# A decoder step on one core: TensorE's attention and search steps put ahead of the weighted sum of the same pick

## Chip, core and metric

The kernel runs on one core of one Trainium2 chip. The metric is the time of one execution on the device, in microseconds; the time of the kernel before is the median of 3 runs, 4178.97 us (4177.4 to 4180.96).

## What is computed

One layer of a decoder for a prompt of 1024 rows and 8 sample sequences of 8 rows. The rows go through a combined projection, an mLSTM group and a dilated attention group, an output projection, and then the part that most of the time goes to, a retrieval over 128 x 128 = 16384 experts of one neuron each. In the reference:

```python
K = PEER_TOPK                                     # 16, for each of 8 heads
s = jnp.einsum('nhpd,pkd->nhpk', qh, sub_keys)    # two times 128 sub-key scores
sv, si = lax.top_k(s, K)
cand = sv[:, :, 0, :, None] + sv[:, :, 1, None, :]
fv, fpos = lax.top_k(cand, K)                     # the best 16 of 256 pairs
gate = jax.nn.softmax(fv, axis=-1)
act = jax.nn.gelu(jnp.einsum('nd,nhkd->nhk', xblk, u_tab[eidx]), approximate=False)
return jnp.einsum('nhk,nhkd->nd', (gate * act), v_tab[eidx])
```

So each row has 8 x 16 = 128 picks, and a pick needs one row of `u_tab` (for a dot product) and one of `v_tab` (for a weighted sum), 1024 numbers each. All is float32.

## The kernel before

Three stages follow each other. Stage 0 makes conditioning rows and bias tables, stage 1 runs the projection and the mLSTM, and stage 3, which begins about 1000 us into the execution, does the attention, the output projection and the retrieval. The change is in stage 3.

**Windows and picks.** Stage 3 works on tiles of 128 rows, 8 of the prompt and a ninth of 64 sample rows. `windows` lists pairs (i, n): in window (i, n) tile i has its 128 picks, while the attention and the search of tile n = i+1 are done beside them. So there are: a first window with no picks of experts (the attention of the sample rows beside tile 0), eight windows i = 0 to 7 with both, and a last one, the 64 picks of tile 8 alone. In windows 0 to 6 tile n has an attention; in window 7 (n = 8) it has a search alone. The same loop over c, the pick, is written out in the program of every engine. It is the order of the statements in that loop that sets each engine's queue; there is no scheduler.

**One pick** of tile i, number g = 128 i + c:

- GpSimd (POOL, L1160) gathers 128 rows of 8 KB (u and v side by side, 1 MB in all) into slot g % 6 of a ring of 6. It waits until the sum of pick g - 6 is done.
- VectorE (DVE, L1631) waits for the slot and multiplies and adds up the u half with the row's input: one number for each of the 128 rows.
- ScalarE (ACT, L1441, L1442, L1445) applies gelu, multiplies by the gate and spreads the 128 weights on the diagonal of a 128 x 128 matrix. There are 4 such matrices; it waits until the sum of pick g - 4 is done.
- TensorE (PE, L1335) waits for the diagonal and multiplies it with the v half, adding up in two banks of PSUM: the weighted sum. Its end frees the slot.

**Steps beside the picks.** `slots(n)` gives the pick at which each step of tile n stands. Attention of a head that begins at pick f (f = 5, 8, 11, ... in windows 0 to 4, and 5, 9, 13, ... in windows 5 and 6): PE makes the scores at f (L1190 against the keys of earlier tiles, L1192 against its own), DVE adds the bias and finds the maximum at f+2 (L1474), ACT takes the exponent at f+3 (L1362, with a table load before it, and one after it for the gelu), PE transposes at f+4 (L1198), ACT copies at f+6 (L1368), PE multiplies with the values at f+7 (L1209, L1210), and DVE scales at f+9 (L1479, L1480). The keys and values of earlier tiles come by SyncE's DMAs, one pair of heads at a time into one buffer each (L1008 and L1014); a load of keys is issued only after the scores of the pair before, and stands in SP's queue behind the load of values, which waits for the products of that pair.

After the heads come a norm over the head outputs, the output projection (PE, two matmuls in each of eight picks, L1234), the residual (DVE, L1512 to L1515, at the fifth and sixth and the ninth and tenth pick after the projection begins), the norm of the result (ACT, L1383 to L1385, with three table loads from there to the next gelu), and then 16 queries (PE L1252, ACT L1391 two picks later, PE L1260 three picks later, DVE five picks later). A query's matmuls wait for the copy of the query before it.

In each pick, DVE and ACT first do the expert's part and then the step of the other tile. PE did the same: first the sum, then the step:

```python
pe.wait_ge(sig["diag"], g + 1)
for half in range(2):
    mm = nc.tensor.matmul(psum[0:r, half], diag[:, g % 4, 0:r], ring[:, g % N_SLOTS, 1, half * 512:(half + 1) * 512], ...)
mm.then_inc(sig["summed"], 1)
```

Of the kernel before, what the change touches and what calls it, by code (L numbers as in the profile page):

```python
# [23 lines left out]
NT = SEQ // P  # L24
# [841 lines left out]
def slots(n):  # L866

    at = {"load": 2}
    if n < NT:
        step = 3 if n < 6 else 4  # L870
        at["head"] = [at["load"] + 3 + step * hh for hh in range(H_B)]
        at["rms"] = at["head"][-1] + 9
        at["turn"] = at["rms"] + 4
    else:
        at["head"], at["rms"], at["turn"] = (), None, 12
    at["out"] = at["turn"] + 4
    at["x1"] = at["out"] + 5
    at["sq"] = at["out"] + 11
    at["h2"] = at["sq"] + 2
    at["turn2"] = at["h2"] + 2  # L880
    first = at["turn2"] + 4
    at["q"] = [first + j * min(45, 99 - first) // 15 for j in range(2 * HEADS)]
    at["found"] = found = [c + 5 for c in at["q"]]
    at["cand"] = [found[2 * hh + 1] + 1 for hh in range(HEADS)]
    at["cand2"] = [c + (2 if c + 1 in found else 1) for c in at["cand"]]
    at["place"] = at["cand2"][-1] + 1
    assert at["place"] + 14 < PICKS
    return at


def stage3(nc, block, sig, mem, psum, const, ins, outs, scratch):
# [76 lines left out]
    def rows_of(i):  # L968
        return NS if i == NT else P

    def picks_of(i):

        return HALF if i == NT else PICKS
# [191 lines left out]
    def _(pe):  # L1165
# [96 lines left out]
        def s_scores(b, p):  # L1262
            m = 3 * b + p
            _, w = S_PIECES[p]
            old = min(512, ROWS - 512 * p)
            if m == 0:
                pe.wait_ge(sig["s_qbd"], 8)
                pe.wait_ge(sig["s_kt"], 2)
            pe.wait_ge(sig[f"s_keys_in{m % 2}"], 16 * (m // 2 + 1))
            if m >= 2:  # L1270
                pe.wait_ge(sig["s_biased"], m - 1)
            for j in range(2):
                for a in range(2):
                    q = s_qbd[:, 2 * a + j, 32 * b:32 * b + 64]
                    mm = nc.tensor.matmul(psum[64 * a:64 * a + 64, m % 2, 0:old], q, s_keys[:, m % 2, 2 * a + j, 0:old], start=j == 0, stop=j == 1)
            if old < w:
                for j in range(2):
                    for a in range(2):
                        q = s_qbd[:, 2 * a + j, 32 * b:32 * b + 64]
                        mm = nc.tensor.matmul(psum[64 * a:64 * a + 64, m % 2, old:w], q, s_kt[a][:, j, DS * b:DS * b + DS], start=j == 0, stop=j == 1)  # L1280
            mm.then_inc(sig["s_s_ps"], 1)

        def s_values(b, g):
            m = 3 * b + g
            t0, n = S_GROUPS[g]
            pe.wait_ge(sig["s_probs_t"], m + 1)
            pe.wait_ge(sig[f"s_vals_in{m % 2}"], 16 * (m // 2 + 1))
            if g == 0 and b >= 1:
                pe.wait_ge(sig["s_o"], b)
            for t in range(t0, t0 + n):  # L1290
                for a in range(2):
                    cols = slice(256 * a, 256 * a + 256)
                    if t < KT_ROWS:
                        mm = nc.tensor.matmul(psum[64 * a:64 * a + 64, 3, 0:256], s_probs_t[:, t, 64 * a:64 * a + 64], s_vals[:, m % 2, t - t0, cols], start=t == 0, stop=False)
                    else:
                        pe.wait_ge(sig["s_new_in"], 16 * (b + 1))
                        mm = nc.tensor.matmul(psum[64 * a:64 * a + 64, 3, 0:256], s_probs_t[0:DS, t, 64 * a:64 * a + 64], s_new[0:DS, cols], start=False, stop=True)
            mm.then_inc(sig["s_o_part"], 1)

        def sample(c):  # L1300
            if c == 0:
                pe.wait_ge(sig["s_raw_in"], 16)
                for n in range(2):
                    for j in range(4):
                        tr = nc.tensor.transpose(psum[:, 0, n * 256 + j * NS:n * 256 + (j + 1) * NS], s_raw[:, n * W_B + j * P:n * W_B + (j + 1) * P], ident[0:NS, 0:NS])
                tr.then_inc(sig["s_turned_ps"], 1)
            for b, first in enumerate(S_FIRST):
                if first <= c < first + 3:
                    s_scores(b, c - first)
                for g, (t0, n) in enumerate(S_GROUPS):  # L1310
                    if c == first + 8 + 3 * g:
                        pe.wait_ge(sig["s_probs"], b + 1)
                        if 3 * b + g >= 1:
                            pe.wait_ge(sig["s_probs_t"], 3 * b + g)
                        for t in range(t0, t0 + n):
                            m = P if t < KT_ROWS else DS
                            tr = nc.tensor.transpose(psum[0:m, 2, (t - t0) * P:(t - t0 + 1) * P], s_probs[:, t * P:t * P + m], ident)
                        tr.then_inc(sig["s_pt_ps"], 1)
                    if c == first + 12 + 3 * g:
                        s_values(b, g)  # L1320

        for i, n in windows:
            at = None if n is None else slots(n)
            picks = picks_of(i)
            for c in range(picks):
                if i is None:
                    sample(c)
                if i is not None:
                    r = rows_of(i)
                    g = i * PICKS + c  # L1330
                    if c == 0 and i >= 1:
                        pe.wait_ge(sig["acc_read"], 2 * i)
                    pe.wait_ge(sig["diag"], g + 1)
                    for half in range(2):
                        mm = nc.tensor.matmul(psum[0:r, half], diag[:, g % 4, 0:r], ring[:, g % N_SLOTS, 1, half * 512:(half + 1) * 512], start=c == 0, stop=c == picks - 1)  # L1335
                    mm.then_inc(sig["summed"], 1)
                if n is not None and n < NT:
                    attention(n, c, at)
                if n is not None:
                    search(n, c, at)  # L1340

    @block.scalar
    def _(act):
# [378 lines left out]
```

## Time and profile before

| what | value |
|---|---|
| time, median of 3 runs | 4178.97 us |
| the profiled execution: its own time, its span | 4189.1 us, 4187.3 us |
| granted TensorE clock, mean | 0.94 |
| DMA, mean over the span | 339 GB/s |
| PE / DVE / ACT / POOL busy, share of the span | 84% / 57% / 39% / 31% |
| largest shares of the chain that ended last | PE weighted sum 21%, DMA of experts 20% |

The span is the time from the first to the last instruction of one profiled execution. That execution took 4189.1 us, 0.24% above the median of the runs shown. A busy share is an average over stages with different limits: what a change in one stage is worth has to be read from that stage. In the section of rows, a window is a stretch of the span in microseconds from its start, and a bracket at the end of a row of the timeline tells how long the engine was idle before the row and what released it.

### The profile page before, as it was taken

To read this page: it belongs to the slowest core of one execution; us is meant where nothing else is said; L and a number is where in the kernel's file an instruction comes from. 1 tells how busy PE (TensorE), PEld (TensorE's weight loads), DVE (VectorE), ACT (ScalarE), POOL (GpSimd) and SP (SyncE) were. 2 spreads that over 40 slices of the span, in tenths; PEclk is the share of its full clock that TensorE was granted. 3 is DMA by queue.
4 is the path that set the end of the run, shared out by engine and by line. 5 is a ranking of instruction groups with operands and counts; after the bars stand their busy time and mean duration, and the time that the engine had idled before them with its cause. 6 is when DMAs were issued, how large, how long until landed. Compare 5 with 4: busy or idle time off the path is not lost.

```text
span 4187.3 us, 38259 instructions
## 1 busy us (share of the span) xinstructions
PE 3507.9 (84%) x12228; PEld 1772.0 (42%) x12228; DVE 2391.9 (57%) x5587; ACT 1616.4 (39%) x4381; POOL 1283.8 (31%) x1204
## 2 busy tenths in 40 slices
PE   7299999678689879978987897898889789889877
PEld 1065665445335334433533453453445344425321
DVE  1044554326548746944874595478548656947744
ACT  0033233123443453454345444443543453333333
POOL 0000000011334433423442343344344334435433
PEclk9699999679799999998998999899999999999999
DMA  9796011875799999999998999899999999999998
GB/s 377 266 339 217 26 44 36 169 251 200 307 377 413 416 358 402 413 364 349 414 416 325 398 413 397 321 401 416 397 386 400 412 386 396 400 368 410 413 408 366
DMA packets 241245, 1420.21 MB, mean 339 GB/s; under 512 B 42963, under 2 KB 65875, under 8 KB 93315
## 3 DMA queue, kind: packets, MB, share of 16 engines
q0 software_dynamic: 168768, 1200.70, 71.4%
q1 hardware_dynamic: 68692, 132.05, 9.9%
q10 hardware_dynamic: 3584, 85.01, 5.7%
q8 instruction: 97, 1.59, 0.2%
q14 instruction: 104, 0.85, 0.1%
HBM read 1385.48 MB, written 98.73 MB: 354 GB/s over the span
## 4 chain that ended last, share of the span: by engine, by line
PE 32%; DMA 25%; DVE 11%; ACT 8%; issue 2%; POOL 1%; SPq 0%; ACTq 0%; POOLq 0%; DVEq 0%
PE psum L1335 21%; DMA mem<-in_experts,mem 20%; DVE mem L1631 6%; PE psum L1252 4%; PE psum L1234 3%; DMA mem<-key_cols 3%; ACT L1441 2%; DVE mem L1497 1%; ACT mem L1445 1%; DVE mem L1496 1%; ACT mem L1442 1%; DMA mem<-qkv_rows 1%; ACT L1362 1%; PE psum L1190 1%; ACT mem L1441 1%
## 5 line engine op out<-in xcount | busy, mean ns | idle before, releaser
L1335 PE MATMUL psum<-mem 128*128 128x512 f32 (+1 forms) x4352 | 2136.4, 624 | 376.9 <-ACT mem L1445 374.8
L1160 POOL DMA_INDIRECT mem<-in_experts,mem x1088 | 1218.0, 1120 | 1882.0 <-PE psum L1335 1814.7
L1631 DVE CUSTOM_DVE_ANT_0 mem<-mem 128x1024 f32<-128x1024 f32 x1088 | 1321.4, 1221 | 705.8 <-DMA mem<-in_experts,mem 694.5
L1335 PEld LDWEIGHTS psum<-mem 128*128 128x128 f32 (+1 forms) x4352 | 774.5, 193 | 1458.0 <-ACT mem L1445 733.4
L1441 ACT ACTIVATE mem<-mem 128x1 f32<-128x1 f32 x1088 | 219.3, 202 | 1579.1 <-DVE mem L1631 1574.6
L1445 ACT ACTIVATE mem<-mem 128x128 f32<-128x128 f32 (+1 forms) x1088 | 434.3, 399 | 35.7
L589 PE MATMUL psum<-mem 128*128 128x512 f32 (+3 forms) x864 | 342.7, 548 | 11.0 <-ACT mem L554 9.8
L1442 ACT ACTIVATE mem<-mem 128x1 f32<-128x1 f32 x1088 | 320.4, 294 | 35.3
L1252 PEld LDWEIGHTS psum<-mem 128*128 128x128 f32 x2304 | 274.4, 191 | 45.1 <-issue 41.7
L1252 PE MATMUL psum<-mem 128*128 128x128 f32 (+1 forms) x2304 | 282.1, 275 | 2.5 <-ACT mem L1391 2.5
L589 PEld LDWEIGHTS psum<-mem 128*128 128x128 f32 (+1 forms) x864 | 148.8, 190 | 178.4 <-issue 164.6
L471 POOL DMA_DIRECT2D qkv_rows<-mem x9 | 5.1, 563 | 563.6 <-DVE mem L811 563.6
L1474 DVE CUSTOM_DVE_ANT_0 mem<-psum,mem 128x128 f32<-128x128 f32 (+7 forms) x64 | 48.4, 757 | 192.3 <-PE psum L1192 180.0
L1496 DVE MAX8 mem<-mem 128x8 f32<-128x128 f32 (+3 forms) x432 | 146.1, 338 | 12.5
L1497 DVE FIND_INDEX8 mem<-mem 128x8 uint32<-128x128 f32 (+3 forms) x432 | 142.3, 330 | 0.0
L1190 PE MATMUL psum<-mem 64*128 64x512 f32 (+3 forms) x160 | 70.0, 545 | 79.9 <-DMA mem<-key_cols 79.9
L1234 PE MATMUL psum<-mem 128*128 128x512 f32 (+1 forms) x288 | 135.5, 594 | 0.0
L616 PEld LDWEIGHTS psum<-mem 128*128 128x128 f32 x1152 | 131.5, 194 | 7.7 <-issue 4.2
L616 PE MATMUL psum<-mem 128*128 128x128 f32 (+1 forms) x1152 | 131.9, 276 | 2.7 <-DVE mem L823 2.7
L315 PE MATMUL psum<-mem 128*9 128x512 f32 x192 | 91.3, 634 | 21.7 <-DMA mem<-in_norm_gain 14.1
L1441 ACT ACT_TABLE_LOAD x80 | 102.6, 1283 | 14.8 <-DVE mem L1631 13.5
L508 ACT ACTIVATE mem<-mem 128x1024 f32<-128x1024 f32 (+1 forms) x9 | 9.4, 1045 | 212.4 <-DMA mem<-in_x 212.4
(259 smaller groups left out, 2577.6 us busy)
## 6 DMA issues: line engine op xcount, KB each, us to landing
out_k_s<-in_cache_k ACTq DMA_DIRECT2D x8, 4080.0 KB, 104.5
out_v_s<-in_cache_v ACTq DMA_DIRECT2D x8, 4080.0 KB, 117.2
mem<-in_w_ada SPq DMA_DIRECT2D x12, 2048.0 KB
mem<-mod_rows SPq DMA_DIRECT2D x34, 512.0 KB
mem<-in_experts,mem POOLq DMA_INDIRECT x1088
mem<-in_keys_t POOLq DMA_DIRECT2D x16, 1024.0 KB, 6.5
mem<-in_vals POOLq DMA_DIRECT2D x16, 1024.0 KB, 7.7
mem<-in_w_in ACTq DMA_DIRECT2D x8, 1796.0 KB, 40.5
```

Of the source, the lines that this page charges most:

```text
L589: mm = nc.tensor.matmul(psum[0:rows, bank, at:at + n], h_ts[i % 2][:, k, 0:rows], w_in[:, k, col:col + n], start=k == 0, stop=k == KD - 1)
L616: mm = nc.tensor.matmul(psum[:, c // 4, c % 4 * P:c % 4 * P + rows], w_in[:, k, O_QK + c * P:O_QK + (c + 1) * P], h_ts[i % 2][:, k, 0:rows ...
L1160: pool.indirect_dma_start(out=ring[:, g % N_SLOTS].rearrange("p a n -> p (a n)"), out_offset=None, in_=ins["experts"][:, :], in_offset=bas ...
L1234: mm = nc.tensor.matmul(psum[0:r, out_banks(n)[half]], turned[:, k, 0:r], w_out[:, k, half * 512:(half + 1) * 512], start=k == 0, stop=k = ...
L1252: mm = nc.tensor.matmul(psum[:, 5, j % 4 * P:j % 4 * P + r], w_q[:, k, j * NKEY:(j + 1) * NKEY], turned[:, k, 0:r], start=k == 0, stop=k = ...
L1335: mm = nc.tensor.matmul(psum[0:r, half], diag[:, g % 4, 0:r], ring[:, g % N_SLOTS, 1, half * 512:(half + 1) * 512], start=c == 0, stop=c = ...
L1441: chain.link(a.activation(act_v[:, c:c + 1], dots[:, c:c + 1], ACT.Gelu))
L1442: chain.link(a.activation(weight[:, c:c + 1], act_v[:, c:c + 1], ACT.Copy, scale=gate[i % 2][:, c:c + 1]))
L1445: a.activation(diag[:, g % 4, 0:r], spread, ACT.Copy, scale=weight[:, c:c + 1]).then_inc(sig["diag"], 1)
L1496: chain.link(v.max(values[:, e:e + 8], src))
L1497: chain.step(v.max_index(places[:, e:e + 8], values[:, e:e + 8], src))
L1631: v.tensor_tensor_reduce(row, row, h2[i % 2], 1.0, 0.0, ALU.mult, ALU.add, dots[:, c:c + 1]).then_inc(sig["dots"], 1)
```

## The change

In PE's loop of stage 3 the two calls of the other tile's steps move ahead of the sum:

```diff
@@ PE, the loop over picks
             for c in range(picks):
                 if i is None:
                     sample(c)
+                if n is not None and n < NT:
+                    attention(n, c, at)
+                if n is not None:
+                    search(n, c, at)
                 if i is not None:
                     r = rows_of(i)
                     g = i * PICKS + c
@@
                     mm.then_inc(sig["summed"], 1)
-                if n is not None and n < NT:
-                    attention(n, c, at)
-                if n is not None:
-                    search(n, c, at)
```

So PE's queue was sum(c), step(c), sum(c+1), step(c+1), and is now step(c), sum(c), step(c+1), sum(c+1). The lines of the sum move from L1335 to L1339. The other engines' queues stay as they are.

PE's queue at the beginning of window 0, before (two rows of L1335 are one sum; L1174 and L1176 are the first step, at pick 2, and L1190 and L1192 the scores of heads 0 and 1, at picks 5 and 8):

```order
L1335 MATMUL psum<-mem 128x512 x6
L1174 MATMUL psum<-mem 128x128 x4
L1176 MATMUL psum<-mem 128x128 x4
L1335 MATMUL psum<-mem 128x512 x6
L1190 MATMUL psum<-mem 128x128
L1192 MATMUL psum<-mem 128x128
L1335 MATMUL psum<-mem 128x512 x6
L1190 MATMUL psum<-mem 128x128
L1192 MATMUL psum<-mem 128x128
```

The same place now:

```order
L1339 MATMUL psum<-mem 128x512 x4
L1174 MATMUL psum<-mem 128x128 x4
L1176 MATMUL psum<-mem 128x128 x4
L1339 MATMUL psum<-mem 128x512 x6
L1190 MATMUL psum<-mem 128x128
L1192 MATMUL psum<-mem 128x128
L1339 MATMUL psum<-mem 128x512 x6
L1190 MATMUL psum<-mem 128x128
L1192 MATMUL psum<-mem 128x128
```

Two sums instead of three stand ahead of the first step; from there on the rows are the same in kind and number, but every sum between two steps is that of one pick earlier.

PE's queue at the end of window 7, before (L1260 is the last of the search's matmuls, for the 64 rows of tile 8; the sums of 64 rows are the last window):

```order
L1335 MATMUL psum<-mem 128x512 x6
L1260 MATMUL psum<-mem 64x128
L1335 MATMUL psum<-mem 128x512 x88
L1335 MATMUL psum<-mem 64x512 x128
```

And now:

```order
L1339 MATMUL psum<-mem 128x512 x6
L1260 MATMUL psum<-mem 64x128
L1339 MATMUL psum<-mem 128x512 x90
L1339 MATMUL psum<-mem 64x512 x128
```

The sum that went missing at the beginning stands behind the last step here, 45 instead of 44.

## Rows read from the trace of the kernel before

**Rows 1.** The page: the span, and busy time of each engine.
```profile
span 4187.3 us, 38259 instructions
PE 3507.9 (84%) x12228; PEld 1772.0 (42%) x12228; DVE 2391.9 (57%) x5587; ACT 1616.4 (39%) x4381; POOL 1283.8 (31%) x1204
```

**Rows 2.** Stretches: us, busy us of five engines, PE clock, DMA share, GB/s. Windows 0 to 7.
```profile
1079.30:4013.40 2934.10, 2529.70 (x8008) 1244.20 (x8008) 1883.64 (x4314) 1290.37 (x3652) 1154.30 (x1023) 0.96 0.98 391
```

**Rows 3.** Stretches of window 2: heads, projection, norm, queries, tail; then the heads of window 5.
```profile
1810.90:1936.60 125.70, 92.36 (x266) 45.37 (x266) 55.23 (x115) 67.03 (x152) 35.61 (x34) 0.86 0.87 334
1936.60:1977.60 41.00, 41.00 (x106) 18.58 (x105) 20.06 (x35) 14.28 (x45) 15.59 (x15) 1.00 0.98 375
1977.60:2001.30 23.70, 17.95 (x41) 7.48 (x39) 10.61 (x16) 12.20 (x31) 9.94 (x9) 0.86 1.01 403
2001.30:2107.80 106.50, 104.45 (x453) 62.55 (x452) 92.97 (x281) 40.23 (x142) 46.55 (x41) 1.00 1.01 414
2107.80:2171.20 63.40, 49.84 (x102) 17.89 (x101) 49.08 (x89) 24.46 (x75) 27.27 (x25) 0.97 1.01 417
2944.90:3078.70 133.80, 115.33 (x382) 60.13 (x382) 67.06 (x130) 78.33 (x176) 47.30 (x41) 0.95 1.00 394
```

**Rows 4.** Who waited for whom, whole span: total us, times, longest us.
```profile
POOL mem L1160 <- PE psum L1335: 1814.7, 964, 16.2
PE psum L1335 <- ACT mem L1445: 374.8, 372, 20.7
DVE mem L1474 <- PE psum L1192: 180.0, 37, 15.2
PE psum L1190 <- DMA mem<-key_cols: 79.9, 14, 11.1
DVE mem L1512 <- PE psum L1234: 77.1, 18, 7.6
```

**Rows 5.** Timeline of window 2, projection to norm: start us, us, engine, line.
```profile
1970.60 1.88 PE L1234 MATMUL psum<-mem 128*128 128x512 f32 x4
...
1972.32 7.04 PE L1335 MATMUL psum<-mem 128*128 128x512 f32 x16
1972.52 0.69 DVE L1512 TENSOR_TENSOR mem<-psum,mem 128x512 f32<-128x512 f32 x1 [5.97 <-PE psum L1234]
...
1981.27 1.28 ACT L1441 ACT_TABLE_LOAD   x1
...
1983.59 8.62 PE L1335 MATMUL psum<-mem 128*128 128x512 f32 x13 [4.23 <-ACT mem L1445]
```

**Rows 6.** Timeline of PE in window 7, the same place.
```profile
3759.70 4.53 PE L1335 MATMUL psum<-mem 128*128 128x512 f32 x6 [4.02 <-ACT mem L1445]
```

**Rows 7.** Timeline of window 2, heads 4 to 6: a wait for keys.
```profile
1872.02 1.99 PE L1335 MATMUL psum<-mem 128*128 128x512 f32 x4 [0.59 <-ACT mem L1445]
...
1875.29 0.49 SPq L1008 DMA_DIRECT2D mem<-key_cols  x1
...
1888.04 1.61 PE L1190 MATMUL psum<-mem 64*128 64x384 f32 x2 [9.31 <-DMA mem<-key_cols]
...
1890.01 3.77 PE L1335 MATMUL psum<-mem 128*128 128x512 f32 x4
...
1894.05 0.94 POOL L1160 DMA_INDIRECT mem<-in_experts,mem  x1 [14.11 <-PE psum L1335]
```

**Rows 8.** Timeline of window 5, one head at 4 picks a head.
```profile
2983.22 0.19 ACT L1362 ACTIVATION_READ_ACCUMULATOR mem<-mem 128x1 f32 x1
...
2984.12 0.39 PE L1210 MATMUL psum<-mem 128*128 128x64 f32 x2
...
2985.74 3.66 PE L1335 MATMUL psum<-mem 128*128 128x512 f32 x4 [1.23 <-ACT mem L1445]
...
2989.19 0.99 PE L1198 MATMUL psum<-mem 128*128 128x128 f32 x7
```

**Rows 9.** Waits of PE alone in the heads of window 2.
```profile
PE psum L1335 <- ACT mem L1445: 14.1, 14, 3.4
```

## The prediction

> **What bounds the kernel now.** I read the page first. PE is busy for 84% of the span [rows 1], but that mixes three stages, so the next view is the stretch from the first sum of window 0 to the last of window 7: 2934.1 us of the 4187.3 in which the DMA engines move 391 GB/s [rows 2]. Then the same view stage by stage, for one window. In its tail, 20 picks and more with no step on PE, 63.4 us hold 25 gathers, 2.54 us each, at 417 GB/s [rows 3]. That is the pace that the transfers allow. The queries run at 414. The heads run at 334 and the projection at 375 [rows 3]; there the transfers starve, because slots come free too late. The share column hardly shows it (0.98 at 375 GB/s), the GB/s do. Had the whole stretch moved 417, it would be 2934.1 x (1 - 391/417) = 183 us shorter. No change of order can give more than that.
>
> Who frees slots late? The table of waits says that POOL waits for sums for 1814.7 us in all, and PE for diagonals for 374.8 us and for keys for 79.9 us [rows 4]. So there are places where PE, which has the sums to make, stands still. Those are the places to look at; the timeline shows three kinds.
>
> **What the change moves.** PE issues the same instructions in the same sequence of kinds. The first sum ahead of the first step is carried behind the last step, so that between two steps stand the sums of one pick earlier. A sum's place in the queue now needs a diagonal that is made one pick sooner. In return, a step is one sum nearer to the start, and the slot that a place in the queue frees is one pick older. Nothing is added: no DMA, no instruction, and the queues of ACT, DVE, POOL and SP do not change. The rule that I draw from it: wherever PE waits in a loop "step on PE, then work on DVE and ACT, then a diagonal, then a sum", the loop now has one more sum of PE inside the time it waits. Four sums in a row take 7.04 us [rows 5], so one is 1.76 us. Where PE waits for a DMA that itself hangs on a step, as many sums stand between the two steps as before, and nothing is won.
>
> **Term A, projection to norm, 8 windows.** The last matmuls of the projection end at 1970.60 + 1.88 = 1972.48 and release DVE, which had been stuck for 5.97 us with later dot products queued behind it. From there the chain goes over the residual, ACT's norm and three table loads, the last at 1981.27, to the next diagonal, and PE goes on at 1983.59 [rows 5]. That is 11.1 us, in which PE has 4 sums (7.04 us) and then idles for 4.23. Now it has 5. The idle time becomes 4.23 - 1.76 = 2.47 us. Window 7, which has no attention, shows the same wait with 4.02 us [rows 6]. The transfers are starved at this place (375 GB/s in the stretch before [rows 3]), so an earlier sum is an earlier gather. 8 x 1.76 = 14.1 us. Bounds: nothing, if the transfers that follow (403 to 414 GB/s) are late anyway; and twice that, 28 us, since the norm over the heads ahead of the projection has a like chain (a wait of 3.4 us is the longest one in the heads [rows 9]).
>
> **Term B, heads of windows 5 and 6.** Here a head takes four picks. PE ends its product at 2984.12 + 0.39 = 2984.51, and the exponent was ready at 2983.41. But the transposes that need the exponent stand behind the sum, the sum behind the diagonal, and the diagonal behind ACT's table load for the gelu: PE idles for 1.23 us, and then makes the sum, in 3.66 us [rows 8]. With the step first, PE takes the transposes and scores at once, and ACT's table load and diagonal run beside them. The wait goes. It comes once a head. Of eight heads I count five, as the transfers are still ahead in the first ones, at 1.0 us: the stretch moves 394 GB/s and has room for 133.8 x (1 - 394/417) = 7.4 us, whatever PE does [rows 3]. 2 windows x 5 x 1.0 = 10 us; bounds 0 and 2 x 7.4 = 14.8.
>
> **Term C, heads of windows 0 to 4.** The large loss here is the wait for keys. PE issues scores at 1888.04 after 9.31 us of idle time; the keys were sent for at 1875.29 [rows 7]. Two sums stand between the product that releases the load and the scores that need it, before and after, so the wait stays. What goes are the small waits between: 0.59 us at the sum just ahead of that product [rows 7]. This kind comes about four times a window in the loops of the keys and values. 5 windows x 4 x 0.6 = 12 us. Bounds: 0; and half of what PE waits there for diagonals without the longest, (14.1 - 3.4) / 2 = 5.4 a window, 27 in all [rows 9].
>
> **Costed at nothing.** The queries: PE is busy for 104.45 of 106.5 us, the transfers run at 414 of 417 [rows 3], so both are full and order is worth nothing. Half of the queries wait for a copy that ACT makes behind the diagonal of the same pick; now that sum stands behind the query. What hides it is that gathers run ahead; if that cover is gone it costs 0.3 to 2 us a query. The tail and the last 64 picks have no steps. Sum: 14.1 + 10 + 12 = 36 us. Against the profiled execution's 4189.1 us that is 4153 us; its median counterpart, 10 us lower, is 4178.97 - 36 = **4143 us**. What is late next is the keys, and the transfers' own 417 GB/s.
>
> **Rivals.** A measurement of this kernel can tell about 0.2%, 8 us, from no change.
>
> *The transfers bound it.* Then the starved places are made good by the bursts after them, and only idle time of PE changes: 4179 us, within 8. For it: in all eight windows the share of the DMA engines is 0.98 [rows 2]. Against it: 334 and 375 GB/s beside 417 [rows 3]. The Trainium skill's page Perfetto Trace Analysis (Roofline) names about 435 GB/s as what the 16 DMA engines of one core give together, and so speaks against any gain by order where that is reached; the trace agrees in the tail, with 417, and not in the heads.
>
> *The keys give it back.* The load of keys of [rows 7] lands 12.75 us after its issue, beside gathers that are released as sums go. If an earlier issue only meets more gathers in flight, term C is nothing and the rest stands: 4179 - 24 = 4155 us. The Trainium skill's page DMA: Bandwidth & Descriptors (Queues, rings and completion order) says that each DMA engine takes turns between its queues, a packet at a time, so that a small load lasts as long as its turns among others' packets; by that rule term C would be 0 here. No row here shows the turns themselves.
>
> *Slots come back one pick later.* During each of the 14 waits for keys [rows 4] the ring now holds one transfer less behind PE: the sum that used to be made ahead of the scores is behind them. If that is what starves the transfers afterwards (POOL waits 14.11 us at one, and the first sum runs for 3.77 us [rows 7]), each wait costs one pick of 2.54 us: 14 x 2.54 = 35.6 us, against A and B with 24: 4179 + 12 = **4191 us, slower**. It decides if scores come at the same time as before. Against it: the place in the queue at which the load is sent for is earlier by the same sum, so that the wait should move as a whole.
>
> *It reaches further.* If A comes at its double and B and C at their upper bounds, 28 + 15 + 27 = 70 us: 4109 us. For it: DVE waits 180 us for scores and 77.1 us for the projection [rows 4], with dot products stuck behind, and each of these waits gets a sum shorter.
>
> **How the numbers follow.** The forecast, with its terms off by up to a half (4125 to 4161), gets 0.53; the keys 0.12; the further reach 0.11; the transfers as the bound 0.13; later slots 0.11. Faster by over 0.2%: 0.53 + 0.12 + 0.11 = 0.76; within: 0.13; slower: 0.11. The range runs from 4110 us, about where the further reach ends, to 4180, so that it takes in half of "no change" and leaves out "slower".
>
> **What would show it.** Right: PE's wait at the norm at about 2.5 us instead of 4.23 in every window; no waits of 1.2 us for diagonals in the heads of windows 5 and 6, and their stretch near 417 GB/s; waits for keys as many and as long as before; DVE's waits for scores and for the projection shorter. Wrong: if those waits shrink and the windows stay as long, the transfers bound it; if the waits for keys grow by 2 us and more each, it is the slots; if PE begins to wait in the queries, the cover that I assumed there is gone.

## The result, and the profile after

The change made the kernel slower: 4207.18 us against 4179.05 us, medians of eight runs each; the ratio is 1.0071, 95% interval 1.0042 to 1.0101. The forecast was 4143 us, and its range ended at 4180.

The profiled execution of the changed kernel took 4192.91 us, the fastest of its eight, and the one of before 4189.1 us, 10 us above its own median. So these two traces show only part of the 28 us. The page, and then the view of stretches (columns as in [rows 2]) of windows 0 to 7, of window 2 (heads, projection, norm, queries), and of the heads of window 5:

```profile
span 4191.1 us, 38259 instructions
...
PE 3516.5 (84%) x12228; PEld 1777.2 (42%) x12228; DVE 2397.0 (57%) x5587; ACT 1617.2 (39%) x4381; POOL 1273.0 (30%) x1204
```

```profile
1071.70:4017.00 2945.30, 2544.14 (x8008) 1252.78 (x8008) 1888.90 (x4314) 1291.35 (x3653) 1144.44 (x1023) 0.95 0.98 390
1805.10:1926.30 121.20, 93.36 (x266) 45.75 (x267) 56.20 (x116) 67.70 (x155) 36.20 (x34) 0.87 0.90 350
1926.30:1967.20 40.90, 40.90 (x106) 18.76 (x105) 19.50 (x32) 15.29 (x45) 16.65 (x15) 1.00 0.97 351
1967.20:1990.70 23.50, 16.54 (x43) 6.54 (x42) 10.93 (x16) 10.41 (x28) 8.72 (x8) 1.00 1.01 417
1990.70:2097.50 106.80, 104.52 (x452) 62.43 (x450) 92.49 (x283) 40.40 (x142) 50.40 (x41) 1.00 1.01 412
2931.50:3070.50 139.00, 115.58 (x383) 60.35 (x383) 66.76 (x129) 78.32 (x174) 44.45 (x41) 0.93 0.94 374
```

The eight windows last 2945.3 us, 11.2 more than [rows 2]. Projection and norm of window 2 take as long as they did [rows 3]. The heads of window 2 are 4.5 us shorter, those of window 5 are 5.2 us longer (139.0 to 133.8), and there the transfers fell from 394 to 374 GB/s. The table of waits, whole span, as in [rows 4]:

```profile
POOL mem L1160 <- PE psum L1339: 1860.5, 1014, 18.0
DVE mem L1631 <- DMA mem<-in_experts,mem: 887.8, 629, 7.7
PE psum L1339 <- ACT mem L1445: 329.4, 328, 20.0
DVE mem L1474 <- PE psum L1192: 113.0, 29, 11.4
PE psum L1190 <- DMA mem<-key_cols: 79.6, 14, 10.1
DVE mem L1512 <- PE psum L1234: 43.3, 17, 4.7
PE psum L1209 <- DMA mem<-qkv_rows: 37.8, 11, 11.8
PE psum L1252 <- ACT mem L1391: 12.4, 14, 2.1
```

The waits that the forecast looked at did shrink: PE for diagonals, DVE for scores and for the projection [rows 4]. Those for keys are as many and as long as before, as forecast. Two grew that it did not look at: PE for values and PE for the copy of a query. These are the two rows of before:

```profile
PE psum L1209 <- DMA mem<-qkv_rows: 9.0, 5, 4.9
...
PE psum L1252 <- ACT mem L1391: 2.5, 3, 1.7
```

One wait for values, in the timeline of window 5 of the changed kernel. The load of the second pair of heads leaves at 2966.85, right behind the products of the first pair:

```profile
2966.43 0.39 PE L1210 MATMUL psum<-mem 128*128 128x64 f32 x2
2966.85 0.37 SPq L1014 DMA_DIRECT2D mem<-qkv_rows  x1
...
2966.95 1.99 PE L1339 MATMUL psum<-mem 128*128 128x512 f32 x4
...
2977.72 0.94 POOL L1160 DMA_INDIRECT mem<-in_experts,mem  x1 [0.69 <-PE psum L1339]
2986.67 2.80 PE L1209 MATMUL psum<-mem 128*128 128x64 f32 x12 [9.22 <-DMA mem<-qkv_rows]
2989.26 0.63 PE L1210 MATMUL psum<-mem 128*128 128x64 f32 x2
2989.69 3.73 PE L1339 MATMUL psum<-mem 128*128 128x512 f32 x4
...
2993.69 0.94 POOL L1160 DMA_INDIRECT mem<-in_experts,mem  x1 [15.03 <-PE psum L1339]
```

The load takes 19.8 us until PE goes on. In the kernel before, the same load leaves at 2984.54 and PE uses it at 2997.24, after 12.7 us and without a wait. So PE not only comes sooner, the load also lasts longer. It is 384 KB in 768 packets of 512 bytes, on the queue q1; the gathers are on q0. Packets and MB of the two queues while the load was under way, 2970 to 2977 in the changed kernel and then 2988 to 2994 in the kernel before:

```profile
q0 software_dynamic: 359, 2.64, 92.5%
q1 hardware_dynamic: 348, 0.18, 8.8%
```

```profile
q0 software_dynamic: 260, 1.88, 80.4%
q1 hardware_dynamic: 776, 0.39, 22.7%
```

In the changed kernel about one packet of the load passes for each one of a gather, and 7 us bring less than half of it. Before, the gathers came more thinly (1.88 MB in 6 us, against 2.64 MB in 7), three packets passed for one of theirs, and 6 us brought nearly all of the load. So in this place the faster pace fills the gaps through which the load used to come. It is the longest of the three such loads in this stretch: they land 9.8, 13.0 and 19.7 us after their issue.

Gathers stop meanwhile: POOL stands idle for 15.03 us between two of them. The stretches of the wait, of the 10 us behind it, and of the first sum among these tell where the time goes:

```profile
2977.50:2986.70 9.20, 0.03 (x1) 0.06 (x1) 2.46 (x4) 5.14 (x10) 0.94 (x1) 0.66 1.03 412
2986.70:2996.70 10.00, 10.00 (x32) 6.81 (x33) 1.96 (x5) 1.82 (x4) 0.94 (x1) 0.63 0.27 86
2989.70:2993.40 3.70, 3.70 (x6) 1.53 (x7) 1.59 (x4) 0.90 (x3) 0.00 (x0) 0.50 0.00 2
```

**In** the wait the transfers run at 412 GB/s: the gathers sent for earlier come in. **Behind** it they run at 86: GpSimd gets no free slot until PE's next sum, which begins at 2989.69 and runs for 3.73 us. The sum at 2966.95 took 1.99. The granted clock of the later one, behind a wait in which PE worked for 0.03 us, is 0.50, the lower of the two levels (1.2 and 2.4 GHz). So the wait is followed by slow work of PE too. The rates over the heads of window 5, in 40 slices, before and after, have that hole:

```profile
GB/s 424 412 419 420 429 421 420 406 424 415 415 418 420 382 379 375 392 413 386 370 336 392 363 348 305 416 387 331 313 401 388 415 427 419 360 407 416 350 419 416
```

```profile
GB/s 418 415 421 422 420 422 417 423 408 424 420 410 403 392 414 413 113 0 182 295 380 405 367 393 404 428 217 198 394 417 375 408 407 420 422 424 420 424 420 415
```

Before, the transfers sag a little everywhere; after, they run at full rate up to the wait and then stop.

### The profile page after: what moved, and what is told of

It is laid out like the page before. It is cut to its first block, busy times and chain, and to the rows that moved or that the text cites. A ratio compares the mean times of both kernels' runs of the same rounds, so it can differ in the third digit from the quotient of the medians.

```text
span 4191.1 us, 38259 instructions
## 1 busy us (share of the span) xinstructions
PE 3516.5 (84%) x12228; PEld 1777.2 (42%) x12228; DVE 2397.0 (57%) x5587; ACT 1617.2 (39%) x4381; POOL 1273.0 (30%) x1204
## 4 chain that ended last, share of the span: by engine, by line
PE 35%; DMA 29%; DVE 9%; ACT 5%; issue 2%; POOL 1%; SPq 0%; ACTq 0%; POOLq 0%; DVEq 0%
PE psum L1339 23%; DMA mem<-in_experts,mem 22%; DVE mem L1631 5%; PE psum L1252 3%; DMA mem<-key_cols 3%; PE psum L1234 3%; DMA mem<-qkv_rows 2%; DVE mem L1497 1%; PE psum L1190 1%; ACT mem L1445 1%; PE psum L1209 1%; DVE mem L1496 1%; ACT mem L1442 1%; PE psum L1275 1%; PE psum L1294 1%
## 5 line engine op out<-in xcount | busy, mean ns | idle before, releaser
L1339 PE MATMUL psum<-mem 128*128 128x512 f32 (+1 forms) x4352 | 2137.4, 626 | 332.3 <-ACT mem L1445 329.4
L1339 PEld LDWEIGHTS psum<-mem 128*128 128x128 f32 (+1 forms) x4352 | 781.0, 193 | 1404.9 <-issue 720.1
L1252 PEld LDWEIGHTS psum<-mem 128*128 128x128 f32 x2304 | 272.9, 192 | 62.9 <-ACT mem L1391 44.7
L1190 PE MATMUL psum<-mem 64*128 64x512 f32 (+3 forms) x160 | 70.2, 546 | 79.6 <-DMA mem<-key_cols 79.6
L616 PEld LDWEIGHTS psum<-mem 128*128 128x128 f32 x1152 | 129.9, 192 | 7.0 <-issue 4.2
L1441 ACT ACT_TABLE_LOAD x80 | 102.6, 1283 | 14.2 <-DVE mem L1631 12.8
L1209 PEld LDWEIGHTS psum<-mem 128*128 128x128 f32 x448 | 67.0, 217 | 75.7 <-issue 75.7
```

Of the source, the lines that this page charges most:

```text
L616: mm = nc.tensor.matmul(psum[:, c // 4, c % 4 * P:c % 4 * P + rows], w_in[:, k, O_QK + c * P:O_QK + (c + 1) * P], h_ts[i % 2][:, k, 0:rows ...
L1252: mm = nc.tensor.matmul(psum[:, 5, j % 4 * P:j % 4 * P + r], w_q[:, k, j * NKEY:(j + 1) * NKEY], turned[:, k, 0:r], start=k == 0, stop=k = ...
L1441: chain.link(a.activation(act_v[:, c:c + 1], dots[:, c:c + 1], ACT.Gelu))
```

## The experiments

All times are medians; each ratio is to runs of the kernel before on the same chip in the same batch. Differences to before in the text are the ratio less 1, times 4179; those between two kernels of one batch are of their medians. "Loads" is PE's wait for keys plus that for values in the profiled execution (before: 79.9 + 9.0 = 88.9).

| kernel | us | ratio to before (95%) | loads, us |
|---|---|---|---|
| whole change | 4207.18 | 1.0071 (1.0042 to 1.0101) | 117.4 |
| e1 search first | 4191.14 | 1.0025 (1.0004 to 1.0046) | 87.5 |
| e2 attention first | 4202.08 | 1.0063 (1.0036 to 1.0091) | 132.0 |
| e3 attention first, windows 5, 6 | 4186.05 | 1.0029 (1.0009 to 1.0049) | 115.0 |
| e4 attention first, windows 0 to 4 | 4188.30 | 1.0031 (1.0009 to 1.0053) | 115.5 |
| e5 search first but queries | 4178.79 | 0.9998 (0.9980 to 1.0016) | 70.4 |
| e6 queries first | 4181.00 | 1.0018 (0.9997 to 1.0039) | 58.3 |
| e7 e3 with half the values | 4155.95 | 0.9942 (0.9923 to 0.9961) | 83.0 |
| e8 before with half the values | 4175.03 | 0.9994 (0.9975 to 1.0014) | 70.6 |
| e9 two buffers | 4109.01 | 0.9839 (0.9817 to 0.9861) | 0.9 |
| e10 two buffers, attention first | 4078.51 | 0.9768 (0.9751 to 0.9785) | 10.5 |
| e11 transposes first, windows 5, 6 | 4179.83 | 1.0011 (0.9995 to 1.0026) | 90.0 |
| e12 one slot less | 4315.42 | 1.0334 (1.0315 to 1.0353) | 62.8 |
| e13 attention first but loads | 4134.08 | 0.9900 (0.9874 to 0.9925) | 78.6 |
| e14 two buffers, whole change | 4078.19 | 0.9777 (0.9752 to 0.9802) | 13.5 |
| e15 two buffers, all but queries | 4078.74 | 0.9767 (0.9743 to 0.9791) | 12.8 |
| e16 loads first | 4236.35 | 1.0161 (1.0132 to 1.0189) | 152.7 |
| e17 releases first | 4156.27 | 0.9939 (0.9915 to 0.9962) | 76.7 |
| e18 transposes first | 4190.57 | 1.0026 (1.0010 to 1.0041) | 105.4 |

The loads of one profile lie between 58.3 and 88.9 us with nothing in the attention changed (before, e1, e5, e6), so they rank only large differences.

### Which part loses (e1 to e4)

Each moves one call ahead of the sum and leaves the other behind; e3 and e4 split the attention by `n >= 6` and `n < 6`. For e1:

```diff
+                if n is not None:
+                    search(n, c, at)
                 if i is not None:
...
                     mm.then_inc(sig["summed"], 1)
                 if n is not None and n < NT:
                     attention(n, c, at)
-                if n is not None:
-                    search(n, c, at)
```

> PE's search step stands ahead of the sum of its pick, its attention step behind it, as before. Theory 'late values' (in windows 5 and 6 the loads of values last longer once transfers run without a pause, and PE waits for them): the search has no such load, and the shorter wait at the norm (2.5 us in place of 4.2) is covered by the five gathers in flight, so within 5 us of the kernel before, 4179 us. Theory 'slots come back later': the loss lies wherever a step stands ahead of a sum, so about half of the loss of the whole change, +10 to +16 us. My prediction's term A alone: -14 us.

> PE's attention step stands ahead of the sum, its search step behind it, as before. 'Late values': as slow as the whole change, +20 to +30 us, with waits of PE for values of 13 to 15 us in each of windows 5 and 6. 'Slots later': the other half, +12 to +18 us.

> The attention step stands ahead of the sum in windows 5 and 6 alone, all else as before. 'Late values': these two windows get longer by 5 to 10 us each as in the profile of the changed kernel (376.4 and 377.6 us against 370.5 and 367.3), windows 0 to 4 stay, so +12 to +20 us, half and more of the loss from two of seven windows. 'Slots later': two of the seven windows with an attention, so +3 to +6 us.

> The attention step stands ahead of the sum in windows 0 to 4 alone, all else as before. 'Late values': the heads of these windows get shorter by 13 us together, as in the profile of the changed kernel, so -5 to -15 us, faster than before. 'Slots later': five of the seven windows with an attention, so +8 to +15 us.

Every part loses: 10 us the search, 12 the attention of windows 5 and 6, 13 that of windows 0 to 4; the three add up to 35, near the 30 of the whole. Neither theory took all four: e2 and e3 came out as "late values" had them, e1 and e4 as "slots" did. So there were at least two causes.

### The queries (e5, e6)

The 16 query products of a window become a function of their own, which stands behind the sum in e5 with the rest of the search ahead, and ahead of it alone in e6:

```diff
+                if n is not None:
+                    search(n, c, at)
                 if i is not None:
...
                 if n is not None:
-                    search(n, c, at)
+                    query(n, c, at)
```

> Search ahead of the sum as in the search-first kernel, but the 16 query products of each window stay behind the sum. Search-first lost 10 us (4191.14 to 4174.07). Theory queries: half of the queries wait for a copy that ACT makes behind the diagonal of the same pick, and PE, with the sum now behind the query, stands still (12.4 to 14.2 us of such waits in the traces, none before) and frees a slot later each time. Then this kernel loses nothing: within 5 us of before, and no wait of PE for that copy in its trace. Rival projection: the loss comes from the output projection and the norm, where each step that PE takes first puts a sum off while five gathers already wait in the ring. Then it loses the same 7 to 12 us.

> The complement: only the 16 query products of each window stand ahead of the sum, all else behind it. Theory queries: 7 to 12 us slower than before, the whole of what search-first lost, with waits of PE for the copy of 12 to 15 us in all. Rival projection: within 4 us of before.

Search without its queries loses nothing (0.9998). The queries alone lose 7.5 us by the ratio, with an interval that just reaches 1. PE's wait for the copy, in e1, e5 and e6:

```profile
PE psum L1252 <- ACT mem L1391: 14.2, 18, 2.1
```

```profile
PE psum L1222 <- ACT mem L1397: 2.5, 3, 1.7
```

```profile
PE psum L1222 <- ACT mem L1397: 10.3, 11, 2.1
```

The stretch of the queries, added up over the eight windows, is 848.2 to 852.7 us in the four kernels whose queries stand first, and 839.3 to 845.2 in all others with six slots. So the loss of the search is that of the queries.

### Values in windows 5 and 6 (e7, e8, e11)

e7 is e3, and e8 the kernel before, with this edit; e11 moves the transposes of windows 5 and 6 alone:

```diff
-            sp.dma_start(v_old[:, 0:n], src.rearrange("(t p) e -> p t e", p=P)).then_inc(sig["v_old_in"], 16)
+            t = n // 2 if n >= 6 and j >= 1 else n
+            sp.dma_start(v_old[:, 0:t], src[0:t * P].rearrange("(t p) e -> p t e", p=P)).then_inc(sig["v_old_in"], 16)
```

The tiles that are not loaded keep the values of an earlier pair, so e7 and e8 leave out a part of the attention and serve for their times alone.

> Attention ahead of the sum in windows 5 and 6 alone, as in the third kernel (which lost 12 us; heads 141.8 and 141.7 us against 133.8 and 135.8 before), and there the load of the values of the second to fourth pair of heads brings half of the tiles only (3 of 6 or 7; the other tiles keep values of an earlier pair). Theory late values: the load lasts about as long as its packets take turns with gathers, and that is now longer than the 8 picks that it has; with half of it PE's waits for values go from 38 us to under 12, the heads of windows 5 and 6 come down to 134 us each or less, and the time to that of the next kernel or up to 6 us below. Rival slots come back one pick later: the heads stay at 139 us and more, 8 us or more above the next kernel in time, since a step that waits still holds a slot.

> The kernel before with the same halved loads of values in windows 5 and 6 (second to fourth pair of heads), to set the kernel with attention first and halved loads beside. PE waits for values there for 9.0 us in all, so both theories expect little: heads of windows 5 and 6 at 130 to 134 us, the time 0 to 6 us below before.

> One buffer as before; in windows 5 and 6 the transposes alone stand ahead of the sum. They wait for ACT's exponent and never for a load; scores and products, which wait for loads, stay behind the sum. Late values: the wait of 1.2 us a head goes, the pace rises to 3.1 us a pick, and the values, sent for only four picks ahead, come late all the same: PE waits 20 us or more for values, heads of windows 5 and 6 at 136 to 144 us, the time 3 to 14 us above before. Slots come back one pick later: no sum is held back by a late load, so heads at 126 to 132 us and the time 5 to 14 us below before.

(The "8 picks" in the first of these are four: a load leaves behind the second head of a pair and is needed by the first head of the next.) Halving the loads is worth 2.5 us with the sum first (e8) and 36 us with the attention first (e3's loss of 12 turned into e7's gain of 24); beside e8, the attention first now gains 19 us. PE's wait for values in e7, where it was 38.3 us in e3, and the heads of window 5 in e7 and in e8 (e3: 141.8 us):

```profile
PE psum L1210 <- DMA mem<-qkv_rows: 13.8, 8, 2.4
```

```profile
2923.30:3050.20 126.90, 111.10 (x381) 57.91 (x382) 67.93 (x130) 78.61 (x176) 43.64 (x41) 0.97 1.02 413
```

```profile
2930.40:3064.70 134.30, 115.42 (x381) 60.51 (x382) 66.61 (x130) 78.06 (x175) 49.06 (x41) 0.95 0.99 388
```

With the load nearly in time, the attention first takes 7.4 us off these heads. The time from issue to landing of the three loads of values in the heads of window 5, in e3 and in e7:

```profile
DMA to landing us min/median/max: 11.0/14.5/19.7
```

```profile
DMA to landing us min/median/max: 10.9/11.8/12.2
```

The Trainium skill's page DMA: Bandwidth & Descriptors (Queues, rings and completion order) has each DMA engine take turns between its queues packet by packet; by that rule a load of half the packets needs half the turns. The packets counted above, about one for one, agree with the turns, and the longest landing, 12.2 us instead of 19.7, goes the way of the rule.

e11 came out as "late values" had it, except that its time, 5 us above before, is not clear of noise. No step that waits for a load has moved, and still PE waits for values, and the heads take 136.5 and 141.8 us:

```profile
PE psum L1213 <- DMA mem<-qkv_rows: 22.7, 3, 10.6
```

A faster pace between the loads is enough to be late at them.

### Loads in time, and the price of a slot (e9, e10, e12)

In e9 and e10 the second and fourth pairs of heads have their keys and values in the rows of the gate and the residual, which lie idle until the projection. The same is done for keys, and in SyncE's queue these loads move ahead of loads of bias rows that they stood behind. A part of the edit:

```diff
+    k_pair, v_pair = (k_old, mod_a), (v_old, x1.rearrange("p (t e) -> p t e", e=P))
...
         def vals_in(n, j):
-            if j >= 1:
-                sp.wait_ge(sig["o_ps"], H_B * n + 2 * j)
+            if j >= 2:
+                sp.wait_ge(sig["o_ps"], H_B * n + 2 * j - 2)
...
+            if 1 <= n < NT:
+                sp.wait_ge(sig["o_ps"], H_B * n + H_B)
             sp.dma_start(x1[0:r], ins["x"][rows_at(n), :]).then_inc(sig["x1_in"], 16)
```

and e12 is, on the kernel before:

```diff
-                if g >= N_SLOTS:
-                    pool.wait_ge(sig["summed"], g - N_SLOTS + 1)
+                if g >= N_SLOTS - 1:
+                    pool.wait_ge(sig["summed"], g - N_SLOTS + 2)
```

> The kernel before (sum first) with two buffers for the keys and two for the values of earlier tiles: the second and fourth pair of heads use the 1024 numbers of the residual's and the gate's rows, which lie idle until the projection. A load then is sent for two pairs ahead instead of after the last use of the pair before. Late loads: PE's waits for keys (50.9 to 97.2 us in the traces so far) fall under 15, the heads of windows 2 to 4 from 118 to 134 us to 112 to 120, the time 20 to 60 us below 4177. Slots come back one pick later: says the same of this one. If the transfers bound the heads anyhow, the time stays within 8 us.

> The same with the attention ahead of the sum in all windows, search behind. With one buffer that cost 25 to 28 us (13 in windows 0 to 4, 12 in 5 and 6). Late loads: with two buffers PE waits for no load, so that the attention first costs nothing: 0 to 25 us faster than the kernel with two buffers and the sum first, heads of windows 5 and 6 at 128 us or less. Slots come back one pick later: a step that is done first holds back a sum and its slot whether or not a load is late, so 8 to 25 us slower than the kernel with two buffers and the sum first.

> The kernel before with GpSimd waiting for the sum of pick g - 5 instead of g - 6, so that five of the six slots are in use: the price of one slot at every pick. Slots come back one pick later: 20 us or more slower, more than half of it in the heads, and PE's and DVE's waits for gathers as in the change (694.5 to 887.8 us) or more. Late loads: under 10 us slower.

With loads in time, the kernel of before is 67 us faster and the attention first is worth 30 us more, where it cost 26 with one buffer. The heads of window 5 in e9 and e10:

```profile
2856.70:2993.80 137.10, 118.62 (x381) 61.64 (x382) 65.38 (x128) 77.60 (x174) 45.42 (x41) 0.93 0.97 378
```

```profile
2850.10:2975.80 125.70, 111.36 (x381) 58.48 (x382) 66.28 (x127) 77.44 (x171) 42.27 (x41) 0.97 1.02 412
```

The order takes 11.4 us off, and e9 shows that more buffers alone do nothing here.

e12 missed both theories: a slot costs 140 us, but not in the heads. Over the eight windows the heads are 898.1 us (before 902.8), the queries 888.8 (843.9) and the norms 227.1 (185.7). Heads, norm and queries of its window 2, for [rows 3]:

```profile
1842.90:1963.40 120.50, 91.10 (x266) 44.90 (x266) 54.61 (x114) 66.36 (x150) 35.46 (x34) 0.89 0.89 342
2007.20:2036.50 29.30, 20.37 (x42) 8.03 (x41) 12.23 (x19) 13.02 (x33) 7.81 (x8) 0.83 0.99 389
2036.50:2147.00 110.50, 105.84 (x453) 62.14 (x451) 91.34 (x280) 39.62 (x139) 45.19 (x41) 1.00 0.99 382
```

### Steps that send for a load and steps that wait for one (e13, e16 to e18)

One buffer again. The attention is called twice, ahead and behind, with a flag; e13 has all but the waiting steps ahead, e16 the waiting steps alone, e17 the scores and products of each pair's second head (the steps that send for the next load), e18 the transposes alone:

```diff
-                if c == first:
+                if c == first and loads == (hh % 2 == 0):
...
-                if c == first + 4:
+                if c == first + 4 and not loads:
...
-                if c == first + 7:
+                if c == first + 7 and loads == (hh % 2 == 0):
```

> One buffer for keys and values as before. In all windows the transposes and the scores and products of the second head of each pair stand ahead of the sum; the steps that wait for a load (the first step of a window, scores and products of the first head of each pair) stay behind it. The whole attention first cost 25 to 28 us. Pace: loads come late because the heads go faster between them, whatever stands behind the waiting step; then what is won between the loads is lost at them, and the time is 0 to 12 us above before, heads of windows 5 and 6 at 135 to 142 us. Held sums: the loss is the finished sum that waits behind a waiting step, so here the time is 5 to 20 us below before.

> The complement of the kernel that was 42 us faster: only the steps that can wait for a load (the first step of a window, scores and products of the first head of each pair) stand ahead of the sum. Held sums: these carry the whole loss, 30 us or more above before, and about 70 if the two parts add up to the 25 to 28 us of the whole attention first; the rate in the ten microseconds after a wait for keys is as low as in the change. If the gain of the other steps only shows because PE comes to the loads at another time: within 15 us of before.

> Ahead of the sum stand only the scores and the products of the second head of each pair, the two steps after which the next load of keys or values is sent for; all else stays behind. A load then has one sum more of PE before the step that waits for it. Lead: 25 to 55 us below before, most of the 42 us of attention_first_but_loads. Held sums (the 42 us came from diagonals no longer waited for ahead of the transposes): within 12 us of before.

> Ahead of the sum stand only the transposes, in all windows: neither the sending nor the waiting step moves. Lead: within 10 us of before (in windows 5 and 6 alone it was 3 us above), so that the two kernels of this call add up to about the 42 us of attention_first_but_loads, and the rest of the whole attention first (25 to 28 us less what this one shows) is the price of a sum held behind a step that waits for a load, at the same lead. Held sums: 15 to 40 us below before.

e13 is 42 us faster, e16 67 us slower. Their waits for keys and values, e13 first:

```profile
PE psum L1190 <- DMA mem<-key_cols: 53.7, 11, 12.8
...
PE psum L1209 <- DMA mem<-qkv_rows: 24.9, 4, 9.5
```

```profile
PE psum L1190 <- DMA mem<-key_cols: 104.2, 16, 9.9
...
PE psum L1209 <- DMA mem<-qkv_rows: 48.5, 11, 10.2
```

I first read this as the held sum, but both kernels also move the steps against each other: between the step that sends for a load and the step that waits for it stand three sums in windows 0 to 4 before and after the change (two for the keys of the third and fourth pair, which stand in SP's queue behind a load of values that waits for the products of the pair two before theirs, [rows 7]); there is one more in e13 and one less in e16. e17, with one sum more and the transposes where they were, gains 25 us by the ratio. e18, with neither a waiting nor a sending step moved, loses 11, the second time that a faster pace between late loads gained nothing. The heads of window 2 in e13 and e16, for [rows 3]:

```profile
1786.20:1894.30 108.10, 87.82 (x266) 44.00 (x266) 53.48 (x112) 65.80 (x149) 39.91 (x34) 0.92 0.96 377
```

```profile
1817.90:1942.90 125.00, 90.94 (x266) 45.23 (x266) 55.43 (x115) 66.92 (x152) 38.12 (x34) 0.88 0.86 336
```

That the lead makes these gains is read from the times. The waits do not prove it: the loads of e13 and e17 in their profiles (78.6 and 76.7 us) lie within the spread of kernels whose attention was not touched. The heads of windows 5 and 6 do not gain from it (133.6 us in window 5 of e13, 133.8 before); the gain lies in windows 0 to 4, of which window 2 is shown above.

e17 and e18 do not add up to e13 (-25 + 11 = -14, not -42). With more lead the faster pace seems to pay, as it does in e10; no run tests this alone. Whole attention (e2, +26 by the ratio) less e18 (+11) leaves 15 us for moving sending and waiting steps together, at an unchanged number of sums between them. That is where the finished sum held behind a waiting step would show. It is a difference of two ratios, each uncertain by 6 to 11 us, and no run isolates it, so its size stays open.

### The whole change with loads in time (e14, e15)

The loops of the whole change, and of e5 with the attention ahead too, on e9:

```diff
                 if n is not None and n < NT:
                     attention(n, c, at)
                 if n is not None:
                     search(n, c, at)
                 if i is not None:
...
                     mm.then_inc(sig["summed"], 1)
+                if n is not None:
+                    query(n, c, at)
```

> The whole change (attention and search first) on the kernel with two buffers for keys and values (4109.01 us with the sum first, 4078.51 with the attention first). The queries' loss is separate from the loads: 7 to 13 us above the kernel with the attention first, 4085 to 4092 us, still 17 to 24 us faster than two buffers with the sum first, PE's waits for the query's copy again 12 to 15 us in all. If the queries lost time only because late loads had emptied the ring: within 4 us of 4078.5.

> As the whole change on two buffers, but the 16 query products of each window stay behind the sum. If the queries are all that search-first loses: 4070 to 4081 us, at or a little below the kernel with the attention first, PE's waits for the query's copy 2.5 us as before. If the projection and the norm lose as well: 4082 us or more.

The very change that lost 30 us is worth 26 here (0.9839 to 0.9777; the medians, 4109.01 and 4078.19, say 31). The queries no longer show in the time (e14 and e15 are equal within the noise), though PE's wait for the copy is there in e14:

```profile
PE psum L1254 <- ACT mem L1393: 13.3, 15, 2.0
```

That is against the expectation. Its queries take 849.0 us, 4 more than in e15, and its projections 4 less (339.0 to 342.7); why the loss is made good with two buffers and not with one stays open.

## Why the prediction was wrong

**What bounds the kernel.** Right: the heads starve. The bound of 183 us holds; e10 and e14 take 97 and 93 of it.

**"What the change moves."** Right in the queue. The step left out is what lies between a load's sending and its use: "as many sums stand between the two steps as before, and nothing is won". As many sums, but each sooner, so the load has less time; and it needs more, as the gathers leave it fewer gaps (in window 5, 19.8 us where 12.7 had been enough). Nothing is won, and something is lost.

**Term A, 14 us: measured at nothing.** Its wait did what was forecast, 4.23 to 2.51 us in window 2 [rows 5], 4.02 to 2.30 in window 7 [rows 6]:

```profile
1971.43 1.99 PE L1339 MATMUL psum<-mem 128*128 128x512 f32 x4 [2.51 <-ACT mem L1445]
```

```profile
3761.37 7.12 PE L1339 MATMUL psum<-mem 128*128 128x512 f32 x12 [2.30 <-ACT mem L1445]
```

The step that failed is "The transfers are starved at this place ..., so an earlier sum is an earlier gather". The projection starves because PE is busy for 41.00 of its 41.00 us [rows 3], not because PE waits; in the norm, where it does wait, transfers ran at 403 GB/s before and run at 417 now. The lower bound, nothing, is what came: e5, with these steps first and the queries behind, is at 0.9998.

**Term B, 10 us: a loss of about 12 (e3).** The waits of 1.23 us went. The room of 7.4 us in a stretch was about right too: 7.4 us came with loads halved (e7 against e8), and 11.4 with two buffers, from a longer stretch (e10 against e9), where the sum had 5 a window. What failed is that no loads were priced in these windows. At the old pace values came in time (12.7 us, no wait); at the new one they took 19.8 us and PE waited 9.22.

**Term C, 12 us: a loss of about 13 (e4).** "So the wait stays" was right (79.9 and 79.6 us). "What goes are the small waits between" was no gain: between loads that are late, they only bring PE to the load sooner (e18). How the 13 us divide between later loads and sums held behind a waiting step stays open.

**"Costed at nothing", the queries: 7 to 11 us** (e6, e1 less e5). The mechanism was named, a query waiting for a copy made behind the diagonal of the same pick. Its cover, "gathers run ahead", held for most and not for all: PE waits for the copy 14 times in the whole span, 3 times before, out of 16 queries a tile, and over the 8 x 16 = 128 queries of the eight windows the loss is 0.06 to 0.09 us each, below the 0.3 to 2 priced for a cover that is gone. No row gives that price.

**The rivals.** Slots one pick later had the right side and came nearest (4191 us). Its place was wrong: a slot is dear in the queries and norms and hardly costs the heads anything (e12), and of its 35.6 us only the open 15 or so of e2 less e18 could be in the heads. "The keys give it back" named what the packets show, a load among more gathers, but for keys and not for values, and it priced it as a lost gain; a late load also costs the starved microseconds behind it. The list of signs had PE's wait in the queries, but not that for values.

## What to carry to other kernels

Before a step is moved on an engine that works in order, list the transfers that are sent for by one step and waited for by another, and count the time between the two at the new pace; a faster pace is worth nothing while those are late. If one side can be moved alone, move the sender ahead and leave the waiter behind: here that took 25 us off with no memory and one flag, 42 with the transposes ahead too, and the opposite cost 67. A second buffer settles it, and then the order that had lost 30 us gained 26.

## What was not expected of the hardware

A wait of PE for a load costs after it ends: 412 GB/s in the 9.2 us, 86 GB/s in the ten behind, with the clock at 0.50 in the sum that frees the next slot. And the same load of 384 KB took at most 12.7 us at the old pace and 19.8 us at the new one, while all transfers together ran at 375 to 420 and 392 to 420 GB/s in the slices around it: the gathers took a larger part of much the same rate, 359 of their packets to 348 of the load where it had been 260 to 776.
